# Attention outputs turned to feature rows by VectorE and GpSimd's transfers in place of TensorE, in a two-layer decoder trunk

## What is computed

```python
proj = x @ w_in                       # gq gk gv gr ga | rq rk rv rg | gate_a gate_b
log_a = log_sigmoid(ga @ gla_w_a2 + gla_b_a) / 16
o_a = gla_chunked(gq / sqrt(128), gk, gv, log_a)           # 4 heads, dk 128, dv 256
o_a = o_a * rsqrt(mean(o_a**2) + LN_EPS) * gla_norm_g
y_a = (silu(gr) * o_a) @ w_pa
o_b = retention_chunked(rotary(rq), rotary(rk), rv, log_gamma)
o_b = (o_b - mean) * rsqrt(var + GN_EPS) * ret_norm_g + ret_norm_b
y_b = (silu(rg) * o_b) @ w_pb
mix = (sigmoid(gate_a + b0) * y_a + sigmoid(gate_b + b1) * y_b) @ w_o
h = layer_norm(ALPHA * h + mix)
f = swiglu(h)                         # layer 0
f = sum over the top 2 of 8 experts   # layer 1
h = layer_norm(ALPHA * h + f)
```

## Time and profile before

| | us |
|---|---|
| median of 3 runs | 1889.14 (1888.65 to 1892.1) |
| the profiled execution | 1885.41 |
| its span, first to last instruction | 1883.4 |
| TensorE busy | 1836.2 (97%) |
| VectorE busy | 1388.6 (74%) |
| ScalarE busy | 1104.6 (59%) |
| GpSimd busy | 7.3 |
| mean granted TensorE clock | 0.990 of full |

### The profile page before, as it was taken

One profiled execution on the slowest core, in us unless ns is written; L12 is line 12 of the kernel. 1 busy time (PEld: TensorE's weight loads), 2 busy tenths in 40 slices (PEclk: granted clock), 3 DMA queues, 4 the chain that ended last, 5 costly groups with the idle time before them and its releaser, 6 DMA issues.

```text
span 1883.4 us, 28533 instructions
## 1 busy us (share of the span) xinstructions
PE 1836.2 (97%) x11042; PEld 1630.3 (87%) x11042; DVE 1388.6 (74%) x1158; ACT 1104.6 (59%) x860; POOL 7.3 (0%) x17
## 2 busy tenths in 40 slices
PE   8999999999999999999999999999999999999996
PEld 8999899999998999998888888888888888888884
DVE  4656566644565566667889889888898888888986
ACT  4544254543444442456776777776777777777773
POOL 0000000000000000000000000000000000000000
PEclk9999999999999999998999999999999999999998
DMA  8525424444535455344999999999989999999992
GB/s 329 201 103 192 158 90 179 158 167 145 183 125 201 155 176 191 128 179 138 361 368 356 359 352 341 365 368 360 360 340 367 353 362 364 337 359 358 356 371 109
DMA packets 75572, 492.81 MB, mean 262 GB/s; under 512 B 9104, under 2 KB 13968, under 8 KB 17616
## 3 DMA queue, kind: packets, MB, share of 16 engines
q1 hardware_dynamic: 73312, 485.79, 69.1%
q10 hardware_dynamic: 1600, 3.31, 0.6%
q0 software_dynamic: 560, 2.29, 0.4%
HBM read 483.66 MB, written 1.05 MB: 257 GB/s over the span
## 4 chain that ended last, share of the span: by engine, by line
PE 58%; DVE 1%; ACT 0%; issue 0%; DVEq 0%; ACTq 0%
PE ps L689 12%; PE ps L691 12%; PE ps L690 12%; PE ps L997 6%; PE ps L999 5%; PE ps L1000 5%; PE ps L983 1%; PE ps L1018 1%; PE ps L1039 0%; PE ps L1040 0%; PE ps L944 0%; PE ps L935 0%; PE ps L847 0%; PE ps L843 0%; PE ps L1027 0%
## 5 line engine op out<-in xcount | busy, mean ns | idle before, releaser
L1716 DVE TENSOR_TENSOR w_lo<-raw,w_hi 128x2048 fp32r<-128x2048 f32 x336 | 763.1, 2289 | 123.4 <-ACT w_hi L1142 121.2
L1142 ACT ACTIVATE w_hi<-raw 128x2048 fp32r<-128x2048 f32 x336 | 637.8, 1919 | 180.9 <-PE ps L1000 98.1
L689 PE MATMUL ps<-hT_hi,w_lo 128*128 128x272 f32 (+1 forms) x1392 | 402.6, 289 | 15.5 <-DVE w_lo L418 11.3
L418 DVE TENSOR_TENSOR w_lo<-raw,w_hi 128x2048 fp32r<-128x2048 f32 (+2 forms) x130 | 277.3, 2142 | 187.9 <-ACT w_hi L411 186.7
L691 PE MATMUL ps<-hT_hi,w_hi 128*128 128x272 f32 (+1 forms) x1392 | 400.8, 288 | 0.0
L690 PE MATMUL ps<-hT_lo,w_hi 128*128 128x272 f32 (+1 forms) x1392 | 400.5, 288 | 0.0
L689 PE MATMUL ps<-w_hi,xg_lo 128*128 128x512 f32 x896 | 357.3, 399 | 1.7 <-DVE xg_lo L2102 1.7
L691 PE MATMUL ps<-w_hi,xg_hi 128*128 128x512 f32 x896 | 351.3, 392 | 0.0
L690 PE MATMUL ps<-w_lo,xg_hi 128*128 128x512 f32 x896 | 351.0, 392 | 0.0
L411 ACT ACTIVATE w_hi<-raw 128x2048 fp32r<-128x2048 f32 (+2 forms) x132 | 234.1, 1782 | 193.3 <-PE ps L691 149.4
L689 PEld LDWEIGHTS ps<-hT_hi,w_lo 128*128 128x128 f32 x1392 | 263.9, 190 | 18.6 <-DVE w_lo L418 10.0
(11 more groups left out here) (278 smaller groups left out, 1819.5 us busy)
## 6 DMA issues: line engine op xcount, KB each, us to landing
raw<-in_dense_units SPq DMA_DIRECT2D x116, 1024.0 KB, 4.9
raw<-in_moe_w_gate SPq DMA_DIRECT2D x112, 1024.0 KB, 7.0
raw<-in_moe_w_up SPq DMA_DIRECT2D x112, 1024.0 KB, 6.9
raw<-in_moe_w_down SPq DMA_DIRECT2D x112, 1024.0 KB, 7.0
raw<-in_dense_units SPq DMA_DIRECT2D x8, 512.0 KB, 4.0
v_tok<-v_blocks SPq DMA_DIRECT2D x64, 64.0 KB, 2.0
raw<-in_dense_units SPq DMA_DIRECT2D x8, 256.0 KB, 6.2
srT<-o_tok ACTq DMA_DIRECT2D x6, 272.0 KB, 4.2
```

Of the source, the lines that this page charges most:

```text
L418: nc.vector.tensor_tensor(w_lo[:, u % HALVES, 0:k * n], raw[:, u % RAW, 0:k * n], w_hi[:, u % HALVES, 0:k * n].bitcast(F32), ALU.subtract) ...
L689: nc.tensor.matmul(dst, l_lo, r_hi, start=start, stop=False)
L1142: return nc.scalar.activation(dst, src, ACT.Copy, **kw)
L1716: tt(w_lo[:, at % HALVES, :], raw[:, at % RAW, :], w_hi[:, at % HALVES, :].bitcast(F32), ALU.subtract).then_inc(lo_ready, 1)
```

## The change

The weight stream has ga's units ahead of gq's, and so have all engines' programs. The transposes on TensorE go, and with them the four local sets. Instead, VectorE turns 32 x 32 blocks of o_tok into o_blocks (in v_tok's memory), GpSimd moves them into oT (in v_blocks's memory) with 16 transfers a branch, 20 in layer 0, and the gating reads oT. In branch r ScalarE makes gain x oT + bias and VectorE has one product for each pair. GpSimd also moves all values of branch g and half of those of branch r; SyncE keeps the other half. In the decay chain VectorE's split and the turn of gv0 come earlier, and ScalarE splits a unit between Exp and Ln. The turn of the last hidden slice stands between the halves of the product before, into memory of its own, and VectorE loads the plan's registers ahead of the last product. The final store is cut in three, and the spills' branches are nested.

```diff
         else:
             add_cols(w_in, COL["gk"])
+        add_cols(w_in, COL["ga"], P)
         add_cols(w_in, COL["gq"])
-        add_cols(w_in, COL["ga"], P)
...
+        flat_v, flat_blocks = (a[:, :, :].rearrange("p a n -> p (a n)") for a in (v_tok, v_blocks))
+        o_blocks = flat_v[:, 0:KT * SEQ].rearrange("p (q t k j) -> p q t k j", q=QUARTERS, k=KT, t=2)
+        oT = flat_blocks[:, 0:KT * SEQ].rearrange("p (b k j) -> p b k j", b=VBLOCKS, k=KT)
...
+        def values_here(eng, l, b):
+            eng.wait_ge(values_landed, 16 * (TURN_DMAS * (l + 1) + TURN_DMAS // 2 * (l + (b == "r"))))
+            if b == "r":
+                eng.wait_ge(late_values_landed, 16 * TURN_DMAS // 2 * (l + 1))
...
         (SyncE)
             def move_values(n):
                 sp.wait_ge(values_turned, n + 1)
-                for q in range(QUARTERS):
...
+                for q in range(QUARTERS // 2, QUARTERS):
                     for c in range(QUARTERS):
-                        sp.dma_start(v_tok[to, 0:2, cols], v_blocks[of, c:VBLOCKS:QUARTERS, :]).then_inc(values_landed, 16)
+                        sp.dma_start(value_rows(q, c), value_blocks(q, c)).then_inc(late_values_landed, 16)
+                    sp.dma_start(meta_value_rows(q), meta_value_blocks(q)).then_inc(late_values_landed, 16)
-            turned_behind = {ends[number[l, f"{b}v1"]] + HALVES - 2 + RAW: 2 * l + (b == "r") for l in range(DEPTH) for b in "gr"}
+            turned_behind = {ends[number[l, "rv1"]] + HALVES - 2 + RAW: 2 * l + 1 for l in range(DEPTH)}
...
-            for t in range(2):
-                sp.wait_ge(normed_ready, 1 + t)
-                sp.dma_start(out[0, t * P:(t + 1) * P, :], y_out[:, t, :]).then_inc(stored, 16)
+            for i, (t, cols) in enumerate(OUT_PIECES):
+                sp.wait_ge(normed_ready, 1 + i)
+                sp.dma_start(out[0, t * P:(t + 1) * P, cols], y_out[:, t, cols]).then_inc(stored, 16)
...
         (GpSimd)
+            def move_values(n, quarters):
+                pool.wait_ge(values_turned, n + 1)
+                for q in range(quarters):
+                    for c in range(QUARTERS):
+                        pool.dma_start(value_rows(q, c), value_blocks(q, c)).then_inc(values_landed, 16)
+                    pool.dma_start(meta_value_rows(q), meta_value_blocks(q)).then_inc(values_landed, 16)
+            def move_outputs(l, b):
+                pool.wait_ge(o_turned, 2 * l + (b == "r") + 1)
+                for q in range(QUARTERS):
+                    to = slice(q * BLOCK, (q + 1) * BLOCK)
+                    for c in range(QUARTERS):
+                        pool.dma_start(oT[to, c:VBLOCKS:QUARTERS, :, :].rearrange("p t k j -> p t (k j)"),
+                                       o_blocks[c * BLOCK:(c + 1) * BLOCK, q, :, :, :].rearrange("p t k j -> p t (k j)")).then_inc(o_landed, 16)
+                    if l == 0:
+                        pool.dma_start(meta_oT[to, :, :].rearrange("p k j -> p (k j)"),
+                                       meta_o_blocks[:, q, :, :].rearrange("p k j -> p (k j)")).then_inc(o_landed, 16)
             for l in range(DEPTH):
+                move_values(2 * l, QUARTERS)
                 pool.wait_ge(scores_out, l + 1)
...
+                move_outputs(l, "g")
+                move_values(2 * l + 1, QUARTERS // 2)
+                move_outputs(l, "r")
...
         (TensorE)
+                    if gated is not None:
+                        pe.wait_ge(gated_lo_ready, gated + k0 // 2 + 2)
...
-                pe.wait_ge(o_ready, 2 * l + 1)
-                transposes(l, ("g_t0", "g_t1"), o_tok, tiles)
-                feature_major(l, "rq", hT_hi, hT_lo, cols, bank_free=(gated_ready, 8 * l + 2))
+                feature_major(l, "rq", hT_hi, hT_lo, cols)
...
-                pe.wait_ge(o_ready, 2 * l + 2)
-                transposes(l, ("r_t0", "r_t1"), o_tok, tiles)
-                feature_major(l, "gtb1", hT_hi, hT_lo, cols, bank_free=(turned_read, l + 1))
+                feature_major(l, "gtb1", hT_hi, hT_lo, cols)
                 for c in range(2):
-                    feature_major(l, f"pb{c}", zT_hi, zT_lo, cols, made_by=("r_t0", "r_t1"))
+                    feature_major(l, f"pb{c}", zT_hi, zT_lo, cols, gated=8 * l + 4)
...
                 pe.wait_ge(hidden_lo_ready, START + k + 1)
                 for i in range(2):
+                    if i and turns:
+                        turn(k + 1)
...
         (ScalarE)
                 step(nc.scalar.activation(fT[:, :, :], fT[:, :, :], ACT.Exp, scale=-1.0))
+                split.upto(ends[number[l, "gv0"]] + 1)
                 settle()
...
+                    if b == "r":
+                        act.wait_ge(o_landed, o_here(l, b))
+                        for k in range(KT):
+                            gain, bias = par_col("ret_norm_g", l * KT + k), par_col("ret_norm_b", l * KT + k)
+                            if l == 0:
+                                nc.scalar.activation(biased[:, k, 0:META], meta_oT[:, k, 0:META], ACT.Identity, scale=gain, bias=bias)
+                            ins = nc.scalar.activation(by_token(biased[:, k, META:T]), o_features(k), ACT.Identity, scale=gain, bias=bias)
+                            if k % 4 == 3:
+                                ins.then_inc(biased_ready, 1)
...
-            def last_down(g):
+            def last_down(g, o):
                 u = NS + (g + 1) * UPG - 2
-                for i in range(2):
-                    hi_of(g, 4 + i, JCH - 1, u + i)
-                turned(g * JCH + JCH - 1, u)
+                hi_of(g, 4, JCH - 1, u)
+                act.wait_ge(hidden_turned, START + g * JCH + JCH)
+                copy(last_hidden(o)[0], TB4).then_inc(hidden_hi_ready, 1)
+                hi_of(g, 5, JCH - 1, u + 1)
...
         (VectorE)
+                split.upto(ends[number[l, "gv0"]] + 1)
                 dve.wait_ge(softplus_ready, l + 1)
                 step(stt(eT[:, :, :], eT[:, :, :], 0.0, fT[:, :, :], ALU.min, ALU.subtract))
-                split.upto(ends[number[l, "gv0"]] + 1)
+                turn_values(l, "g", 0, ahead=1)
                 settle()
...
-                turn_values(l, "g", 0, ahead=1)
                 turn_values(l, "g", 1)
...
-                    dve.sem_inc(o_ready, 1)
+                    for t in range(2):
+                        ins = nc.vector.transpose(o_blocks[:, :, t, :, :].rearrange("p q k j -> p k q j"),
+                                                  o_tok[:, t, :].rearrange("p (k q i) -> p k q i", k=KT, q=QUARTERS))
+                    if l == 0:
+                        ins = nc.vector.transpose(meta_o_blocks[:, :, :, :].rearrange("p q k j -> p k q j"),
+                                                  o_tok[0:BLOCK, 2, :].rearrange("p (k q i) -> p k q i", k=KT, q=QUARTERS))
+                    ins.then_inc(o_turned, 1)
...
+                    if b == "g":
+                        dve.wait_ge(o_landed, o_here(l, b))
...
+                        for k in range(4 * c, 4 * c + 4):
+                            gain, z = par_col("gla_norm_g", 2 * l + k % 2), srT[:, k, :]
+                            if b == "g":
+                                if l == 0:
+                                    stt(z[:, 0:META], meta_oT[:, k, 0:META], gain, z[:, 0:META], ALU.mult, ALU.mult)
+                                ins = stt(by_token(z[:, META:T]), o_features(k), gain, by_token(z[:, META:T]), ALU.mult, ALU.mult)
+                            elif k % 2:
+                                pair = (slice(None), slice(k - 1, k + 1), width(l))
+                                ins = tt(srT[pair], srT[pair], biased[pair], ALU.mult)
...
+                lo(4, u)
+                dve.wait_ge(hidden_hi_ready, START + k + 1)
+                tt(a_lo, ps[0][:, 2, :].rearrange("p (k s) -> p k s", s=P), a_hi.bitcast(F32), ALU.subtract).then_inc(hidden_lo_ready, 1)
+                lo(5, u + 1)
...
-            last_down(EXPERTS - 1)
             n_groups, spill = load_plan(dve)
+            last_down(EXPERTS - 1, 1)
```

More of the change, by code:

```diff
@@ L646, in _, with spilled @@
             n_groups, spill = load_plan(sp)
-            for s in range(SPILLS):
+            def spilled(s):
                 with sp.If(n_groups > s):
@@ L780, in norm_sums @@
                     nc.tensor.matmul(pt[:, 2, cols], still[:, 0, META:META + P], still[:, 0, cols], start=True, stop=True)
[L782 to L789, removed]
-                            last = nc.tensor.transpose(pt[:, k, c:c + n], src[0:n, t, f:f + P], ident[0:n, 0:n])
-                    fill(last)
             def key_tokens(l, name, made_by, keys):
@@ L901, in _ @@
                     feature_major(l, f"rv{c}", hT_hi, hT_lo, slice(0, T))
-                feature_major(l, "pa0", zT_hi, zT_lo, cols, made_by=("g_t0", "g_t1"))
+                feature_major(l, "pa0", zT_hi, zT_lo, cols, gated=8 * l)
                 key_tokens(l, "r_kt", rotated, lambda h: keys_of["r"][:, h, :])
@@ L984, in turn, with down @@
```

(26 more changed lines are left out.)

146 lines of the change are left out of this document (71 added, 75 removed).

## The result

The changed kernel takes **1917.94 us** (median of 4 runs, 1916.5 to 1920.94), the kernel before, timed beside it, 1888.89 (1886.51 to 1892.1). The ratio is 1.0156 with a 95% interval of 1.0144 to 1.0169: slower by 29 us, where +1.7 was forecast and the range ended at 1906.

What follows compares the result with a forecast made beforehand. TensorE, busy 97% of the span, was taken as the bound. Terms -13.9 + 19.3 + 4.3 - 7.6 + 0 - 0.7 = +1.4, rounded up to +1.7 on 1889.1, gave 1890.8 us, range 1874 to 1906.

Steps and rivals of the forecast that it cites:

- transposes gone: TensorE's transposes of each branch, waits included, all on the path: four windows, -13.9 us.
- waits before rk and pb0: TensorE stalls for the weight units behind the gating: 4.9 and 0 in branch g, 10.5 and 3.9 in r, +19.3 us.
- waits before pa1 gone: Sharing the r values between two queues removes both TensorE waits before pa1: -5.9 us, plus -1.7 for a slow stretch.
- tail: Behind the last hidden halves: wait shortened by 0.4, three output pieces 0.3, together -0.7 us (-2.3 to +0.5).
- The landing: Output transfers from GpSimd's last issue to landed, ahead of the gating: taken as 1.5 us.
- The allowance: Dense stage: with ScalarE or VectorE held up, TensorE has at most one set of 96 matmuls, 12.15 or 11.37 us.
- part 4: ga before gq and the reordered decay chain, followed up to gv1's second unit: 0 us (-2 to +1.5).
- The clock: Slow 1.2 GHz stretches behind TensorE's new stalls, two and a half of 1.7 us each: +4.3 us (0 to 7).
- the nested branches: The spills' branches nested, said to lie beside longer waits: 0 us.
- rival B: GpSimd's queue is the bound through slower issues: 1900 us at 0.67 per issue, near 1919 at 0.93; chance 0.23.
- C: Rival: the shared value move fails and the waits before pa1 stay, 1898 us; chance 0.10.
- part 2: What replaces the transposes: turn, moves, gating, then the queued weight split; stalls +19.3 us and slow clock +4.3.

Runs made afterwards that it cites:

- experiments 2 and 4: Experiment 4 varied the value moves: all r values back on SyncE in the changed kernel, 1925.14 us; the kernel before with the value moves alone changed, 1883.07 us.
- Experiment 2: The changed kernel with SyncE holding the weight load that falls into the output moves, and those behind it, until the attention outputs have landed: 1900.38 us.
- `sync_values`: The changed kernel with all r values on SyncE's queue again, the g values staying with GpSimd: 1925.14 us.
- experiment 1: The changed kernel with ScalarE and VectorE splitting the next set's two weight units before they wait for the attention outputs: 1888.23 us, ratio 0.9996 to the kernel before.
- `before_values`: The kernel before with the value moves alone changed (g values on GpSimd, r values half on each queue): 1883.07 us, ratio 0.9970.
- the mended kernel: The changed kernel with units split ahead of the gating, weight loads held while the outputs move, and gq before ga: 1872.12 us, ratio 0.9912.
- `before_values_tail`: The kernel before with the value moves and the tail's changes, nothing of the outputs or of ga: 1878.85 us, ratio 0.9950.

## Why the prediction was wrong

In spans, from the starts of TensorE's sets in the two traces, with my term beside each. The last row is what is left of the sum and was not measured by itself:

| part | forecast | by the traces |
|---|---|---|
| transposes gone | -13.9 | -13.9 |
| waits before rk and pb0 | +19.3 | +39.7 |
| waits before pa1 gone | -5.9 | -5.9 |
| ga, gq and the decay chain | 0 | +7.6 |
| tail | -0.7 | -3.3 |
| the rest, mostly stretches at the lower clock | +2.6 | +7.6 |
| sum | +1.4 | +31.8 |

**The landing** is the step that failed most: "Landing: ... I take 1.5", the term between GpSimd's last issue and the gating, was 5.6 us in the first chain. It came from the earlier trace rows: SyncE's value moves. Those rows are of a stretch in which SyncE, the only issuer of weight loads, was busy with these very moves, so that no weights were in flight once its last load had landed at 200.7; from 203 to 211 the DMA engines were 29 to 35% busy. The move to GpSimd took that cover away: SyncE goes on loading, and the outputs share the DMA engines with it. I had put "both ends" on the issue time, 0.4 to 0.93, and none on the landing. The issue was the forecast's 0.54 exactly. The Trainium skill (DMA: Bandwidth & Descriptors, "Issuing engines are not separate DMA queues") says that transfers of all issuers run on the same DMA engines and interleave, whoever issued them. The windows and landings of experiments 2 and 4 agree, 1.9 us alone against 6.2 beside weight loads. I had weighed only its other half, that several issuers save only the time to initiate, usually small beside the transfer. The "usually small" does not hold here, where sharing the value moves was worth 5.6 and 7.2 us. Experiment 2 prices the contention at 17.6 us.

**The allowance** was named, "one set of 96 matmuls", and then not applied to part 4: with ga first, the set in front of a full unit is one of 24. I followed the chain behind z instead and took 0 (-2 to +1.5). The part cost 7.6, undone 8.1; 4.7 us of it is the wait before gq in the two layers, less 1.0 for that before z.

**The clock.** Stretches at a granted clock of 0.50, the 1.2 GHz level, number ten up to 900 us where there were five, one behind each of the four long waits and others behind smaller ones. The windows from the end of each long wait to the end of its stretch:

```profile
170.50:175.80 5.30, 5.29 (x23) 5.30 (x24) 3.81 (x2) 2.21 (x2) 0.00 (x0) 0.50 0.84 227
301.58:305.50 3.92, 3.92 (x17) 3.92 (x18) 1.94 (x1) 3.91 (x6) 0.00 (x0) 0.50 0.77 272
721.01:725.34 4.33, 4.33 (x19) 4.33 (x20) 2.74 (x2) 2.15 (x2) 0.00 (x0) 0.50 0.79 219
840.13:844.81 4.68, 4.68 (x22) 4.68 (x23) 2.69 (x2) 3.88 (x6) 0.00 (x0) 0.50 0.82 298
```

Set against the pace of the earlier trace rows, 23 matmuls where there is time for 42 and so on, they lose 2.4, 1.8, 2.1 and 2.1 us, 8.3 in all; the one behind pa1 is gone in return. I had 4.3 for two and a half such stretches of 1.7. So the number was off, as I had no stall for rk in layer 1, and each was a little longer than the one that I took as the measure.

**The tail** came out better by two mistakes. I charged the registers, to VectorE's time in front of the last w_lo. But they are its queue's work, and that runs ahead: in the changed kernel the four loads and their register operations go on from 1886.9 to 1889.6, while VectorE does a w_lo until 1888.8 and a product until 1889.4, and the next w_lo starts with 0.39 us idle:

```profile
1888.71 0.68 DVE L2068 TENSOR_TENSOR a_sl<-ps,g_sl 128x512 f32<-128x512 f32 x1
1889.78 2.29 DVE L1770 TENSOR_TENSOR w_lo<-raw,w_hi 128x2048 fp32r<-128x2048 f32 x1 [0.39 <-PE ps L1045]
```

That is the most that they can have cost, and TensorE does not feel it: the wait of 1.81 us before the last product is gone altogether. And "the nested branches lie beside longer waits: 0" was wrong: what they lay beside, within 0.1 us, was the store, which the same change shortens. That the forecast of -0.7 for this part missed on the good side is no merit of it.

**The rivals.** The outcome lies where rival B ended, but by another mechanism: its "slower issue" did not happen. C was refuted in the changed kernel, by its trace and by `sync_values`; in the kernel before, the wait of layer 1 did stay. None of the rivals was a transfer that lands late, although the question was there to ask: what else will be on the DMA engines when this transfer is issued from another queue? The mechanism behind all of part 2, that the weight split queues behind the new wait, was right, and experiment 1 shows that undoing it gives back 29.7 us.

Open: what made GpSimd pause in `before_values` is not known. In the part around ga, the place of ga and the order of the decay chain were not tried apart. Experiments 1 and 2 were not tried one without the other inside the mended kernel, so how much holding the weights still brings there was not measured. Whether branch r could do without its 6.4 us of ScalarE work before the gating was not tried either.

## What to carry to other kernels

Where two engines feed a third from a short ring of buffers, put the refilling of the ring ahead of any new wait in their programs, and no further ahead than slots are already free; here one line in each of two programs was worth 30 us. A duration from issue to landing belongs to the traffic of its stretch: moving a transfer to another queue also sets free the queue that used to be silent beside it. And before pricing the shortening of a last step, look at which other engine ends within a tenth of a microsecond of it.

## What was not expected of the hardware

A transfer of 64 KB in 1 KB rows took 1.9 us from issue to landing with the DMA engines half used and 6.2 (up to 7.8) with them full of 1 MB loads. Register loads of VectorE's queue, some 0.63 us apart, ran almost entirely under instructions that were already running: four of them left 0.39 us of idle time at most. In the kernel before, three branches whose bodies were not entered took 3.4, 4.8 and 5.2 us on TensorE's queue, which therefore reached its drain 5.5 us behind the last result, as late as the 512 KB store beside it was through. About 1 us behind the start of each, the DMA rows have a packet of 16 KB of the kind "instruction"; that the branch waits for it is likely, but not shown. GpSimd, whose issues followed each other every 0.54 us, paused once in the middle of them in every kernel that gave it such moves: 1.1 us in most, 3.4 and 3.8 in `before_values_tail` and `before_values`.
